# A mixture-of-experts kernel: scattered rows come back by accumulating DMAs, few rows are zeroed, VectorE writes a layer's first pick

## The reference

```python
scores = sigmoid(xt @ w_router)
biased = scores + b_router
# the best of 4 groups, and in it the best 2 of 4 experts: idx, w
combine = sum(one_hot(idx, 16) * w[..., None], axis=1)
for e in range(16):
    hdn = silu(xt @ w_gate[e]) * (xt @ w_up[e])
    y = y + combine[:, e:e + 1] * (hdn @ w_down[e])
h = h + g2 * y
```

## Time and profile before

| | |
|---|---|
| median of 3 runs | 948.86 us (945.38 to 950.93) |
| the profiled execution | 949.5 us |
| its span, first to last instruction | 947.7 us |
| TensorE busy | 860.3 us (91%) |
| VectorE / ScalarE / GpSimd busy | 321.6 / 171.3 / 144.2 us |
| mean granted TensorE clock | 0.96 of full speed |
| moved by DMA | 320.88 MB |

### The profile page before, as it was taken

One profiled execution on the slowest core, in us unless ns is written; L12 is line 12 of the kernel. 1 busy time (PEld: TensorE's weight loads), 2 busy tenths in 40 slices (PEclk: granted clock), 3 DMA queues, 4 the chain that ended last, 5 costly groups with the idle time before them and its releaser, 6 DMA issues.

```text
span 947.7 us, 11949 instructions
## 1 busy us (share of the span) xinstructions
PE 860.3 (91%) x4387; PEld 479.2 (51%) x4388; DVE 321.6 (34%) x580; ACT 171.3 (18%) x339; POOL 144.2 (15%) x230
## 2 busy tenths in 40 slices
PE   6996899999999699999799868899699999999983
PEld 3785344444445454455354427684455555555531
DVE  2748568768822311111111033350311111111102
ACT  2100111221101212222110112250322212212001
POOL 0022000000002511111100151400611111101005
PEclk9998899999999799999999899999899999999997
DMA  9999999899689889999999995425369999399991
GB/s 321 387 347 373 360 389 375 326 379 381 269 249 392 335 351 420 404 420 422 422 422 423 418 409 177 173 85 221 133 239 424 408 405 423 142 407 419 424 415 53
DMA packets 68548, 320.88 MB, mean 339 GB/s; under 512 B 7918, under 2 KB 8049, under 8 KB 43166
## 3 DMA queue, kind: packets, MB, share of 16 engines
q1 hardware_dynamic: 62330, 308.62, 82.1%
q0 software_dynamic: 3824, 7.97, 2.2%
q10 hardware_dynamic: 2356, 3.76, 1.3%
HBM read 315.50 MB, written 15.20 MB: 349 GB/s over the span
## 4 chain that ended last, share of the span: by engine, by line
PE 71%; DMA 15%; DVE 5%; POOL 3%; issue 2%; ACT 1%; SPq 1%; POOLq 0%; ACTq 0%; DVEq 0%
PE bank L699 12%; PE bank L888 12%; DMA ring<-in_moe_w_up 8%; PE bank L906 8%; PE bank L875 8%; PE bank L737 6%; PE bank L850 5%; DMA part<-outs 4%; PE bank L640 3%; PE bank L1123 3%; POOL h L1914 2%; DVE part L1479 2%; DMA outs<-arena,row_id 2%; PE bank L1078 1%; PE bank L898 1%
## 5 line engine op out<-in xcount | busy, mean ns | idle before, releaser
L888 PE MATMUL bank<-ring,arena 128*64 128x256 f32 x1088 | 131.0, 396 | 18.5 <-DMA ring<-in_moe_w_up 18.5
L888 PEld LDWEIGHTS bank<-ring,arena 128*64 128x64 f32 x1088 | 83.0, 142 | 67.0 <-issue 36.2
L1479 DVE SCALAR_TENSOR_TENSOR part<-ring,cpad,part 128x1024 f32<-128x1024 f32 x84 | 109.0, 1297 | 21.2 <-DMA ring<-in_w_mod 16.4
L1711 DVE TENSOR_TENSOR arena<-bank,arena 128x256 f32<-128x256 f32 x34 | 21.0, 618 | 276.1 <-PE bank L888 276.1
L699 PE MATMUL bank<-ring,xnT 128*128 128x512 f32 x256 | 112.4, 597 | 0.0
L906 PE MATMUL bank<-ring,arena 128*64 128x512 f32 x480 | 109.3, 596 | 3.2 <-issue 3.2
L875 PE MATMUL bank<-ring,arena 128*64 128x512 f32 x480 | 106.3, 595 | 0.0
L850 PE MATMUL bank<-arena,y 128*128 128x128 f32 x544 | 70.8, 293 | 10.2 <-POOL arena L1860 10.2
L699 PEld LDWEIGHTS bank<-ring,xnT 128*128 128x128 f32 x256 | 48.7, 192 | 61.9 <-issue 61.9
L850 PEld LDWEIGHTS bank<-arena,y 128*128 128x128 f32 x544 | 67.6, 206 | 24.0 <-issue 24.0
L875 PEld LDWEIGHTS bank<-ring,arena 128*64 128x64 f32 x480 | 33.1, 137 | 60.2 <-issue 60.0
(11 more groups left out here) (297 smaller groups left out, 864.8 us busy)
## 6 DMA issues: line engine op xcount, KB each, us to landing
ring<-in_moe_w_up SPq DMA_DIRECT2D x64, 1024.0 KB, 12.7
ring<-in_moe_w_gate SPq DMA_DIRECT2D x56, 1024.0 KB, 14.7
ring<-in_moe_w_down SPq DMA_DIRECT2D x56, 1024.0 KB, 15.5
ring<-in_w_mod SPq DMA_DIRECT2D x48, 1024.0 KB, 12.1
ring<-in_ret_w_in SPq DMA_DIRECT2D x24, 1024.0 KB, 11.5
ring<-in_w_mod_kv SPq DMA_DIRECT2D x8, 1024.0 KB, 13.0
ring<-in_ret_w_out SPq DMA_DIRECT2D x8, 1024.0 KB, 9.2
outs<-in_zeros SPq DMA_DIRECT2D x2, 2048.0 KB, 18.9
```

What stands on the lines that cost most here:

```text
L888: ins = pe.matmul(bank[1 + f][e * 64:(e + 1) * 64, 0:256], xgT[:, k, e * 64:(e + 1) * 64], w(2 + e, k)[:, f * 256:(f + 1) * 256], start=(k ...
L1479: ins = dve.scalar_tensor_tensor(o, w[:, k, :], c, o, ALU.mult, ALU.add)
```

## The change

Four things are different.

- SP no longer writes zeros, and the input `zeros` is gone. GpSimd zeroes `part[:, 0, :]` and scatters it four times per layer, 128 rows each, at `back_id`: for each of the 512 rows its own number if the token's choice is in the last pair, and a number outside the buffer if not. VectorE works out `back_id` with five small instructions.
- VectorE writes the first `pick` of a layer in one instruction of 128x256, right behind the table. GpSimd writes the later ones. In each pass of its loop it now scatters first, then adds 64 to the slot numbers and writes the pick of a further round of the same pair, whether there is one or not, then makes `row_id`; a pair's first pick is written ahead of its loop.
- The two readbacks add into `h` themselves (`accum_op=ALU.add`). Both write the same bytes of `h`, so the second is issued when the first has landed. The eight adds are gone, and VectorE's last adds wait for `back_in`.
- A scatter raises a further semaphore, `issued`, for which GpSimd waits after each.

```diff
-            sp.dma_start(outs[0], t["zeros"].to_broadcast([2 * SEQ, D])).then_inc(cleared, 16)
...
-                    sp.dma_start(outs[1], t["zeros"].to_broadcast([2 * SEQ, D])).then_inc(cleared, 16)
...
-                        if last:
-                            pe.wait_ge(S["picked"], u)
-                        else:
-                            pe.wait_ge(S["picked"], u + 1)
+                        pe.wait_ge(S["picked"], u + pair + (PAIRS - 1) * l + (0 if last else 1))
...
+                dve.wait_ge(placed, l + 1)
+                four = [P, TT, 2, SLOTS]
+                dve.tensor_tensor(pick.rearrange("p t (e s) -> p t e s", e=2), slots0.unsqueeze(1).unsqueeze(1).to_broadcast(four),
+                                  place[:, :, 0:2].unsqueeze(3).to_broadcast(four), ALU.is_equal).then_inc(S["picked"], 1)
...
+                own.step(dve, dve.tensor_tensor(in_last[:], in_last[:], cst[:, C_BACK:C_BACK + 2 * TT].rearrange("p (t f) -> p t f", f=2), ALU.mult))
+                dve.tensor_scalar(back_id[:], in_last[:], float(NO_ROW), None, ALU.add).then_inc(back_ready, 1)
...
-                        dve.wait_ge(back_added, 8 * (l + 1))
+                        dve.wait_ge(back_in, 32 * (l + 1))
...
+                def next_slots(u, pair):
+
+                    hold(S["info_done"], u + 2)
+                    hold(S["slots_ready"], PAIRS * l + pair + u + 1)
+                    pool.tensor_scalar(slot_id[:], slot_id[:], float(SLOTS), None, ALU.add).then_inc(S["slots_ready"], 1)
+                    hold(S["slots_ready"], PAIRS * l + pair + u + 2)
+                    pick_of(pick, slot_id[:], place_two).then_inc(S["picked"], 1)
+                    hold(S["picked"], (PAIRS - 1) * l + pair + u + 2)
+
+                def rows_out(u):
+
+                    hold(S["row_ready"], u + l + 2)
+                    hold(S["yg_ready"], u * 2 + 2)
+                    scatter(yg, row_id[:, 0:1], S["scattered"])
+                    hold(S["issued"], u + 5 * (l + 1))
+
+                def row_ids(u):
+
+                    pool.wait_ge(cleared, 64 * (l + 1))
+                    hold(S["scattered"], u * 16 + 16 * (l + 1))
+                    hold(S["info_ready"], u + 1)
+                    pool.tensor_scalar(row_id[:], info[:, 0:1], float(NO_ROW), None, ALU.add).then_inc(S["row_ready"], 1)
...
+                for j in range(2 * TT):
+                    scatter(part[:, 0, :], back_id[:, j // 2, j % 2:j % 2 + 1], cleared)
+                    issue_done(j + 1)
+                with pool.Fori(bound(slice(0, 1), 0) if l else 0, bound(slice(1, 2), 1)) as u:
+                    rows_out(u)
+                    next_slots(u, 0)
+                    row_ids(u)
...
-                for f, dst in enumerate((acc, part)):
-                    pool.dma_start(dst[:], outs[l].rearrange("(t p f) n -> f p t n", p=P, f=2)[f]).then_inc(back_in, 16)
-                pool.wait_ge(back_in, 32 * (l + 1))
-                for n in range(2):
-                    for tt in range(TT):
-                        c = slice(n * 512, (n + 1) * 512)
-                        for f, src in enumerate((acc, part)):
-                            pool.tensor_tensor(h[:, tt, c], h[:, tt, c], src[:, tt, c], ALU.add).then_inc(back_added, 1)
-                            pool.wait_ge(back_added, 8 * l + 4 * n + 2 * tt + f + 1)
+                for f in range(2):
+                    pool.dma_start(h[:], outs[l].rearrange("(t p f) n -> f p t n", p=P, f=2)[f], accum_op=ALU.add).then_inc(back_in, 16)
+                    pool.wait_ge(back_in, 32 * l + 16 * (f + 1))
```

More of the change, by code:

```diff
@@ L43 @@
 C_TOKEN = C_OVER + ROUNDS - 1
-C_DECAY = C_TOKEN + TT
+C_BACK = C_TOKEN + TT
+C_DECAY = C_BACK + 2 * TT
 NO_ROW = 1024
@@ L180, in build_kernel @@
         info = sb("info", [P, 2])
+        back_id = sb("back_id", [P, TT, 2], I32)
+        in_last = sb("in_last", [P, TT, 2])
         row_id = sb("row_id", [P, 1], I32)
@@ L1862, in pick_of, with scatter @@
                     return ins
[L1864 to L1866 removed]
+                def scatter(src, ids, landed):
+                    pool.indirect_dma_start(out=outs[l], out_offset=bass.IndirectOffsetOnAxis(ap=ids, axis=0), in_=src,
+                                            in_offset=None, bounds_check=2 * SEQ - 1, oob_is_err=False, engine_sem=S["issued"]).then_inc(landed, 16)
                 def bound(at, least):
                     return pool.value_load(bounds[l][0:1, at], min_val=least, max_val=ROUNDS * PAIRS * (l + 1))
+                def next_slots(u, pair):
[15 more added lines that the diff above has]
+                    pool.tensor_scalar(row_id[:], info[:, 0:1], float(NO_ROW), None, ALU.add).then_inc(S["row_ready"], 1)
                 pool.tensor_scalar(row_id[:], ones[:, 0:1], float(NO_ROW), None, ALU.mult).then_inc(S["row_ready"], 1)
@@ L1873, in experts @@
                     pool.memset(yg, 0.0).then_inc(S["row_ready"], 1)
-                pool.wait_ge(cleared, 16 * (l + 1))
+                pool.memset(part[:, 0, :], 0.0).then_inc(zeroed, 1)
                 pool.wait_ge(bounds_ready, l + 1)
                 pool.wait_ge(placed, l + 1)
+                pool.tensor_copy(slot_id[:], slots0)
+                pool.tensor_copy(place_two[:], place[:, :, 0:2]).then_inc(S["slots_ready"], 1)
                 pick_of(pick_last, slots0, place[:, :, NE - 2:NE]).then_inc(picked_last, 1)
-                pool.tensor_scalar(slot_last[:], slots0, float(SLOTS), None, ALU.add).then_inc(S["slots_ready"], 1)
@@ L1879, in experts, with issue_done @@
-                with pool.Fori(0, PAIRS - 1) as pair:
-                    begin = bound(bass.ds(pair, 1), 0)
+                pool.tensor_scalar(slot_last[:], slots0, float(SLOTS), None, ALU.add).then_inc(picked_last, 1)
+                pool.wait_ge(picked_last, 2 * l + 2)
+                pool.wait_ge(back_ready, l + 1)
+                pool.wait_ge(zeroed, l + 1)
+                def issue_done(j):
+                    if l:
+                        hold(S["issued"], bound(slice(0, 1), PAIRS) + 5 + j)
+                    else:
+                        pool.wait_ge(S["issued"], j)
@@ L1881, in experts @@
+                for j in range(2 * TT):
[5 more added lines that the diff above has]
+                    row_ids(u)
+                with pool.Fori(1, PAIRS - 1) as pair:
+                    begin = bound(bass.ds(pair, 1), 1)
                     end = bound(bass.ds(pair + 1, 1), 1)
-                    hold(S["slots_ready"], PAIRS * l + pair + begin + 1)
@@ L1883, in experts @@
-                    hold(S["info_done"], begin + 1)
                     pool.tensor_copy(slot_id[:], slots0)
                     pool.tensor_copy(place_two[:], place[:, :, bass.ds(pair * 2, 2)]).then_inc(S["slots_ready"], 1)
+                    hold(S["slots_ready"], PAIRS * l + pair + begin + 1)
+                    pick_of(pick, slot_id[:], place_two).then_inc(S["picked"], 1)
+                    hold(S["picked"], (PAIRS - 1) * l + pair + begin + 1)
                     with pool.Fori(begin, end) as u:
[L1888 to L1898, removed]
@@ L1900, in experts @@
+                        rows_out(u)
+                        next_slots(u, pair)
+                        row_ids(u)
                 first = bound(slice(PAIRS - 1, PAIRS), PAIRS - 1)
-                hold(S["row_ready"], first + l + 2)
-                hold(S["yg_ready"], first * 2 + 2)
-                scatter(yg)
+                rows_out(first)
                 hold(S["scattered"], first * 16 + 16 * (l + 1))
```

24 lines of the change are left out of this document (16 added, 8 removed).

## The result

The changed kernel takes 934.57 us (median of 4, 933.18 to 938.03) against 948.75 for the kernel before on the same chip: a ratio of 0.986, 95% interval 0.982 to 0.990. In a later set, on a chip where the kernel before took 950.61, it took 936.13 (0.986, 0.983 to 0.989). The profiled run after took 935.13 with a span of 933.4, against 947.7 before: 14.3 us less.

A forecast was written before the change was run, and what follows sets the result against it. The chain was 71% TensorE and 15% DMA; only TensorE's stalls for GpSimd or its DMAs at layer starts and ends counted. 949.5 - 9.0 - 7.0 = 933.5, less 0.6 for the median: 933, range 925 to 953.

The forecast's parts named there:

- Zeros, nothing: SP's two 2 MB zero writes leave its queue: costed at nothing, below 1 us if they help.
- First pick, -9.0 in two terms: At both layers' starts, VectorE's pick shortens TensorE's gap by 7.6 us and the less fallen clock gives 1.4.
- The gain reaches the end in full: The 9.0 us from the layers' starts last, because the saturated weight stream starts earlier by the same amount.
- Rival B: Layer starts gain nothing lasting: 4 to 5 us return as waits for `up`; 938, or 942 with layer 1's; 14%.
- GpSimd's head, nothing: Before pair 0, GpSimd's four zero scatters and added work cost 0; pair 1's pick is ready about 341.5, wanted about 346.
- Rival C: GpSimd's head is 12 us longer, pair 1's pick comes 8 us late in both layers: 949; 8%.
- Readback, -7.0: At both layers' ends, accumulating readbacks replace eight GpSimd adds: -7, the middle between -10.0 and -4.
- the dear end: Readback's costly bound: each byte costs the engines twice, down weights come about 3 us later; -1.7 and -2.2, sum -4.
- Rival A: Accumulates at the layers' ends take 20.0 us each, in series, slower than before: 959; turning at 17.6 each; 20%.

The follow-up runs named there:

- the nine profiles: Profiles of the changed kernel and seven variants with the same work between table and readback: 432.8 us there on average (431.2 to 434.9), against 439.0 before.
- the pick experiment: Changed kernel, but GpSimd instead of VectorE writes the first pick of each layer again: 940.45 us, ratio 0.991 to the kernel before.
- the plain pair: Changed kernel, but with two plain readbacks issued together and eight adds on GpSimd again: 938.04 us, ratio 0.990 to the kernel before.

## Why the prediction was right

The forecast was 933 (925 to 953); measured 934.57 and 936.13. The mechanism was right in its two main parts, the waits for GpSimd at the layers' starts and the adds behind the readbacks. That the sum came within 2 us is in part luck: the starts won 1.5 us less than forecast and the readbacks 0.7 more, and the first row of the table above, 1.2 us, belongs to no part of the change.

- *Zeros, nothing*: right. With them back in their old form the time is the same (935.61 against 934.57).
- *First pick, -9.0 in two terms*: the first, 7.6 for the shorter gap, measured 3.45 + 3.06 = 6.5. From the table to TensorE's gather it took 1.45 and 1.76 us, not the 0.93 and 1.24 read off ScalarE: the prediction sized TensorE's entry by another engine's. The second, 1.4 for the clock, measured 0.13 + 0.81 = 0.94. Together 7.5 at the gate products (9.0 forecast). The clock gave so little because it was down again within the short gap (0.57 on average, 0.50 behind it).
- *The gain reaches the end in full*: not contradicted, and not shown to the last microsecond. Of the 7.5 us, 5.7 and 4.5 are left at the readbacks' issues in the two profiles of the changed kernel, but 6.2 of 7.3 by the average of the nine profiles, and the part that the pick experiment takes away at the starts, 4.2 us, is missing at the end too (4.5 to 5.9). Rival B, by which the gain of layer 0 or of both layers comes back as longer waits for `up`, is out as a whole: in layer 0 those waits are 8.5 and 9.1 us in the two profiles after, against 9.3 before. In layer 1 the wait is 1.8 and 0.4 us against 0.5, so a microsecond may go back there.
- *GpSimd's head, nothing*: right. The four zero scatters are issued 1.74 to 2.01 us apart, and pair 1's pick is ready at 340.2:

```profile
320.20 1.21 POOL L1876 DMA_INDIRECT outs<-part,back_id  x1 [0.93 <-POOL slot_last L1914]
322.21 0.99 POOL L1876 DMA_INDIRECT outs<-part,back_id  x1 [0.79 <-DMA outs<-part,back_id]
...
338.45 1.71 POOL L1871 TENSOR_SCALAR arena<-slot_id,place_two 128x64 f32<-128x64 f32 x4 [0.20 <-POOL place_two L1936]
```

  It was wanted at 346.6, where pair 1's gather starts, and TensorE waits for GpSimd nowhere. Rival C is out.
- *Readback, -7.0*: -7.7 by the trace (-5.7 by the second profile), -3.5 by the medians of the plain pair. By the trace the size is right, the split is not: -2.3 and -5.5 where the working had the layers nearly alike. What I missed is the prefetch of the next block, which exists in layer 0 only; holding it back brings 10.0 us for the second accumulate, near layer 1's 8.8. Of the dear end, "each byte costs the engines twice" is close (1.75 times, alone), but "the down weights come 3 us later" did not happen with one transfer outstanding: TensorE awaits them for 2.03 and 0.46 us (2.85 and 0.76 in the second profile) against 1.88 and 1.37. With two it did happen, at 3.6 to 6.2 us. The Trainium skill, in "Collectives: The Full Stack", section "The bandwidth ceiling: the fold count and why AG ≠ RS ≠ AR", states for a ReduceScatter between cores that its add needs two source reads and that it delivers half as fast as an AllGather. The engines' time of the accumulate here is near that (5.9 against 3.3 us); the landings show less, 8.9 against 6.1.
- *Rival A* (20 us each, turning at 17.6): the four took 14.9, 13.2, 16.1 and 8.8. The first ones came within 3 us of the turning point, and the second ones took less than the first in both layers.

## What to carry to other kernels

A transfer at a kernel's or a layer's end is priced by what is in flight beside it: look at which queues still issue there, hold back what is wanted later, and keep one transfer outstanding, not two, while another engine still waits for weights. Eight adds that GpSimd did on the path (10.7 us) were well replaced here by accumulating DMAs, even at nearly twice the engines' time. A stall taken away ahead of a stream of weights lasted for the most part here, as the stream started earlier too; to tell whether a microsecond of it was lost took more than two profiles, since two of one kernel differ by as much.

## What the runs showed of the hardware

- An accumulating DMA of 1.05 MB from DRAM into SBUF, alone: 8.8 to 8.9 us to its landing and 5.9 us of 16 engines' time, against 6.1 and 3.3 for a plain one.
- Beside weights that fill the engines the same accumulate takes 13 to 16 us. With the next block's prefetch held back, the second one of layer 0 takes 8.6 to 10.0.
- TensorE's granted clock was at 0.57 on average in a gap of 1.70 us, and cost the next 32 products 2.2 to 2.55 us; with fillers in the gap it stayed at 1.00. After an idle wait of 6.19 us it was at 0.56, and 16 products took 6.36 us instead of 3.65.
- Two readbacks outstanding at once, at least one of them accumulating, made TensorE wait 1 to 4 us longer for the other queue's weights than accumulates one at a time; two plain ones did not. GpSimd's queue had 37 to 42% of the engines then, against 29%.
